# A two-block network on one core: low parts of a projection moved to VectorE, the experts' sums started from the residual, a semaphore for the number of rounds

## The reference

```python
# block 1, behind its first feed-forward (D_FF 2816)
h = rms_norm(x, norm_mix)
p = h @ w_in                       # 1024 x 3328; the last 1792 columns are u
# RWKV-7 mix of those columns
u = u + (token_shift(u) - u) * mu  # token_shift: the row of the token before, zeros ahead
...
# block 2, behind its attention: x is the residual, t its norm
y = sum over 16 experts: gate_e * ((silu(t @ w1e) * (t @ w3e)) @ w2e)   # 2 of 16 per token
x = x + g * y                      # g: a row of 1024 gates from the modulation
out = x * rsqrt(mean(x * x) + 1e-6) * final_g
```

## Time and profile before

| | |
|---|---|
| Median of 3 runs | 1210.21 us (1205.83 to 1211.66) |
| Profiled execution | 1211.14 us, its span 1209.3 us |
| Mean granted TensorE clock | 0.982 of full |
| TensorE busy | 1146.7 us (95%) |
| VectorE busy | 604.2 us (50%) |
| ScalarE busy | 446.9 us (37%) |
| GpSimd busy | 51.6 us (4%) |
| HBM read | 252.25 MB |

### The profile page before, as it was taken

The page is one execution under the profiler, slowest core; times in us unless marked ns, Lnnn a source line. Parts: engine busy times, 40 slices in busy tenths (PEclk is TensorE's granted clock), DMA queues, the critical chain, the costliest instruction groups (busy, mean ns, idle before and its releaser), DMA issues.

```text
span 1209.3 us, 20587 instructions
## 1 busy us (share of the span) xinstructions
PE 1146.7 (95%) x8864; PEld 922.0 (76%) x8864; DVE 604.2 (50%) x767; ACT 446.9 (37%) x532; POOL 51.6 (4%) x37
## 2 busy tenths in 40 slices
PE   6999998998989998999999999999979799999996
PEld 6999997997768747999999999888878544444443
DVE  5544546798534275654456481477486511111114
ACT  6333345752441125434335242466553411111112
POOL 0000000340032000000000000000000000000000
PEclk9999999998999999999999999999999899999998
DMA  9655556452664743655654352433225799999991
GB/s 342 213 175 188 194 177 190 140 166 82 231 255 142 272 166 121 196 187 177 200 179 139 105 175 71 140 105 105 73 97 183 278 364 423 421 421 421 421 422 56
DMA packets 119845, 254.32 MB, mean 210 GB/s; under 512 B 6097, under 2 KB 91361, under 8 KB 107234
## 3 DMA queue, kind: packets, MB, share of 16 engines
q1 hardware_dynamic: 118578, 248.61, 57.6%
q10 hardware_dynamic: 1200, 4.71, 1.1%
HBM read 252.25 MB, written 1.06 MB: 209 GB/s over the span
## 4 chain that ended last, share of the span: by engine, by line
PE 87%; DVE 7%; ACT 3%; issue 1%; DMA 1%; SPq 0%; DVEq 0%; ACTq 0%
PE ps L652 52%; PE ps L633 33%; ACT arena L1309 2%; DMA ring<-in_ffn_gate 1%; DVE ring_r L1804 1%; PE ps L1101 1%; ACT arena_r L1309 1%; DVE arena L2074 1%; DVE arena L1950 1%; ACT L1309 1%; DVE arena L1946 1%; DVE arena L1951 0%; DVE arena L1956 0%; DVE arena L1962 0%; PE ps L640 0%
## 5 line engine op out<-in xcount | busy, mean ns | idle before, releaser
L652 PE MATMUL ps<-hall_r,arena_r 128*128 128x256 f32 x1664 | 301.3, 283 | 2.9 <-DVE hall_r L1810 2.9
L1804 DVE TENSOR_TENSOR ring_r<-ring,arena_r 128x2048 fp32r<-128x2048 f32 x90 | 205.9, 2291 | 194.0 <-ACT arena_r L1309 191.9
L652 PE MATMUL ps<-arena_r 128*128 128x256 f32 (+1 forms) x1280 | 290.1, 322 | 7.4 <-DVE ring_r L1804 4.2
L652 PEld LDWEIGHTS ps<-hall_r,arena_r 128*128 128x128 f32 x1664 | 257.7, 189 | 5.1 <-issue 2.1
L1309 ACT ACTIVATE arena_r<-ring 128x2048 fp32r<-128x2048 f32 x100 | 190.6, 1914 | 159.8 <-PE ps L652 153.7
L652 PE MATMUL ps<-hall_r,ring_r 128*128 128x256 f32 x880 | 247.5, 281 | 0.0
L1309 ACT ACTIVATE arena<-ps 128x512 f32<-128x512 f32 (+4 forms) x147 | 86.1, 597 | 409.5 <-PE ps L652 211.0
L652 PEld LDWEIGHTS ps<-arena_r 128*128 128x128 f32 x1280 | 211.3, 189 | 26.2 <-DVE ring_r L1804 4.4
L633 PE MATMUL ps<-arena 64*64 64x32 f32 (+7 forms) x2360 | 204.7, 301 | 3.7 <-issue 1.5
L633 PEld LDWEIGHTS ps<-arena 128*64 128x64 f32 (+3 forms) x2360 | 135.7, 146 | 72.8 <-issue 62.8
L652 PEld LDWEIGHTS ps<-hall_r,ring_r 128*128 128x128 f32 x880 | 169.0, 192 | 0.9
(11 more groups left out here) (228 smaller groups left out, 922.5 us busy)
## 6 DMA issues: line engine op xcount, KB each, us to landing
ring<-in_w_in SPq DMA_DIRECT2D x35, 1024.0 KB, 5.2
ring<-in_w_exp_gate SPq DMA_DIRECT2D x32, 1024.0 KB, 11.6
arena<-in_w_exp_down SPq DMA_DIRECT2D x32, 1024.0 KB, 11.2
ring<-in_w_mod SPq DMA_DIRECT2D x24, 1024.0 KB, 5.6
ring<-in_ffn_gate SPq DMA_DIRECT2D x22, 1024.0 KB, 5.4
ring<-in_ffn_up SPq DMA_DIRECT2D x22, 1024.0 KB, 5.3
ring<-in_ffn_down SPq DMA_DIRECT2D x22, 1024.0 KB, 5.0
ring<-in_w_exp_up SPq DMA_DIRECT2D x16, 1024.0 KB, 14.1
```

Source lines behind the costliest of these rows:

```text
L652: m = pe.matmul(out_, w[i], h[j], start=start and i + j == 0, stop=stop and j == 1, skip_group_check=group)
L1804: tt(lo(n), slot(n), hi(n), ALU.subtract).then_inc(S("w_lo"), 1)
```

## The change

Three things, and what they bring with them.

- **Projection.** All thirteen low parts are VectorE's. `copy_out(j)` for j < 7 now writes (1 - mu) times the bank into the target tile, in two operations of 256 columns, with `mu_rest` = 1 - mu made once at the start; `shift(j)` adds mu times the bank's columns, one to the left, straight from PSUM. `ubuf` and `ushift` go. TensorE therefore also waits for `shift(j - 4)` before it writes a bank again. Two high parts have other places, and high parts 8 and 9 another order on ScalarE.
- **Residual.** The four clearing matmuls become four with the identity and x, so the banks start from x. `y_e` is multiplied by g as it is copied, in two operations on VectorE; ScalarE's copy goes. The scatter goes half by half of the columns and signals each of its four banks. ScalarE squares each bank as it is ready, VectorE's final product reads the banks, and the final gain comes by a broadcast DMA into `gb[:, 0]`, issued on SP behind the first pair's loads. Each half of the output is stored when it is ready.
- **Rounds.** "rounds" leaves the group `dve_tail` and has a semaphore of its own.

```diff
--- before.py
+++ after.py
@@ -169,15 +169,15 @@
             "pe_rms": [("sbo_ms", 2), ("y_mean", 2), ("y_var", 2)],
-            "pe_tail": [("dft_1", 4), ("heads_ss", 4), ("dft_2", 2), ("route_bias", 1), ("logits_t", 2), ("logits", 1), ("places", 2), ("moe_sum", 2),
-                        ("final_gain", 1)],
+            "pe_tail": [("dft_1", 4), ("heads_ss", 4), ("dft_2", 2), ("route_bias", 1), ("logits_t", 2), ("logits", 1), ("places", 2), ("moe_sum", 4),
+                        ],
...
                          ("route_w", 1), ("route_shift", 1), ("n5_inv", 2),
-                         ("route_max", 1), ("chosen", 1), ("route_diff", 1), ("tables", 10), ("rounds", 1)],
+                         ("route_max", 1), ("chosen", 1), ("route_diff", 1), ("tables", 10)],
@@ -297,7 +297,7 @@
-            block = (23, 21, 17, 25, None, 23, 25, None, 25, None, 7, 25, 5)[j]
+            block = (23, 21, 17, 25, None, 23, 25, None, 4, 25, 7, None, 5)[j]
@@ -372,8 +372,13 @@
         x_wa, x_g, t_w, s_g = (A(3, 256, 256 * j) for j in range(4))
-        ubuf = A(4, 1028).rearrange("p (b f n) -> p b f n", b=2, f=2)
-        ushift = A(4, 512, 1028).rearrange("p (f n) -> p f n", f=2)
+        mu_rest = small[:, 56:70]
...
+        def mixed(j, f):
...
+            tile = 2 * RW_ORDER[j] + f
+            return {12: x_wa, 13: x_g}.get(tile, rw_x[tile // 4 * 4][:, tile % 4, :] if tile < 12 else None)
@@ -402,6 +407,7 @@
         w_end = small[:, 0:16].rearrange("p (k c) -> p k c", k=4)
+        halves_ss, half_mean = small[:, 0:4], small[:, 4:6]
@@ -552,14 +558,16 @@
             expert_pair(0, 0, True)
+            sp.wait_ge(*W("x4_done", 4))
+            sp.dma_start(gb[:, 0, :], a["rows"][:, 0:D].broadcast_to([P, D])).then_inc(S("final_gain"), 16)
...
                 expert_pair((i % (E // 2)) * 2, i)
-            sp.wait_ge(*W("final", 2))
             for t in range(TT):
+                sp.wait_ge(*W("final", t + 1))
@@ -579,12 +587,6 @@
             pool.memset(r_scan.rearrange("p (c n) -> p c n", n=CH)[:, :, 0:1], 0.0).then_inc(S("reset_mask"), 1)
...
-            pool.memset(ubuf[:, :, :, 0:1], 0.0).then_inc(S("ubuf_zero"), 1)
-            for j in range(5, 10):
-                pool.wait_ge(*W("win_hi", j + 1))
-                pool.tensor_tensor(lo_cols(N_WIN + j), cols(N_WIN + j), win_hi(j), ALU.subtract).then_inc(
-                    S("win_lo_p"), 1)
@@ -614,9 +616,8 @@
             pool.wait_ge(*W("w_used", N_AO + 2))
-            pool.memset(y_e, 0.0).then_inc(S("y_kept_v"), 1)
+            pool.memset(y_e, 0.0).then_inc(S("y_kept_v"), 2)
             pool.memset(pick_t, 0.0).then_inc(S("pick_t"), 1)
-            pool.memset(zero_blk, 0.0).then_inc(S("zeros"), 1)
@@ -759,12 +760,11 @@
                 n = N_WIN + j
-                if 5 <= j < 10:
-                    pe.wait_ge(*W("win_lo_p", j - 4))
-                else:
-                    pe.wait_ge(*W("win_lo_v", j + 1 if j < 5 else j - 4))
+                pe.wait_ge(*W("win_lo_v", j + 1))
...
                     pe.wait_ge(*W("win_copied", j - 3))
+                if 4 <= j < 11:
+                    pe.wait_ge(*W("shifted", j - 3))
@@ -1206,9 +1206,10 @@
-            pe.wait_ge(*W("zeros", 1))
-            for b in range(4):
-                m = mm(ps[:, 4 + b, :], zero_blk, cst[:, 0:512], stop=False, group=True)
+            pe.wait_ge(*W("x4_done", 4))
+            for t in range(TT):
+                for h in range(2):
+                    m = mm(ps[:, 4 + 2 * t + h, :], ident, x[:, t, h * 512:(h + 1) * 512], stop=False, group=True)
@@ -1222,15 +1223,14 @@
-                pe.wait_ge(*W("y_kept_v", i + 1))
-                pe.wait_ge(*W("y_kept_a", i + 1))
                 pe.wait_ge(*W("pick_t", i + 1))
-                for t in range(TT):
-                    for h in range(2):
+                for h in range(2):
+                    pe.wait_ge(*W("y_kept_v", i * 2 + (h + 1)))
+                    for t in range(TT):
...
                                stop=False, group=True)
-                    if sem:
-                        m.then_inc(S(sem), 1)
+                        if sem:
+                            m.then_inc(S(sem), 1)
@@ -1267,8 +1267,7 @@
                 pe.wait_ge(*W("picked", i + 2))
-                pe.wait_ge(*W("y_kept_v", i + 1))
-                pe.wait_ge(*W("y_kept_a", i + 1))
+                pe.wait_ge(*W("y_kept_v", i * 2 + 2))
@@ -1298,10 +1297,6 @@
-            for h in range(2):
-                m = mm(ps[:, h, :], ones[0:1, :], row_f[:, h * 512:(h + 1) * 512])
-            m.then_inc(S("final_gain"), 1)
@@ -1410,12 +1405,14 @@
                 if j < 7:
-                    if j >= 2:
-                        act.wait_ge(*W("shifted", j - 1))
-                    elif j == 0:
-                        act.wait_ge(*W("ubuf_zero", 1))
-                    o = ubuf[:, j % 2, :, 1:T + 1]
-                elif j < 11:
+                    if j == 0:
+                        act.wait_ge(*W("mu_rest", 1))
+                    for g in range(2):
+                        tile = 2 * RW_ORDER[j] + g
+                        m = f(mixed(j, g), bank[:, g, :], ACT.Copy, scale=mu_rest[:, tile:tile + 1])
+                    m.then_inc(S("win_copied"), 1)
+                    return
+                if j < 11:
@@ -1455,13 +1452,13 @@
             high_in(7)
+            high_in(8)
...
             copy_out(6)
-            high_in(8)
+            high_in(9)
             copy_out(7)
-            high_in(9)
@@ -1743,8 +1740,6 @@
-            act.wait_ge(*W("y_kept_v", 1))
-            act.sem_inc(S("y_kept_a"), 1)
@@ -1763,17 +1758,22 @@
                 f(hs_t, ps[:, 0, :].rearrange("p (k n) -> p k n", k=4), ACT.Copy).then_inc(S("hs_t"), 1)
-                act.wait_ge(*W("w_used", i * 12 + (N_EXP + 12)))
-                f(y_e[:, 0:512], ps[:, 2, :], ACT.Copy).then_inc(S("y_kept_a"), 1)
...
             fetch(ACT.Sqrt)
-            for t in range(TT):
-                act.wait_ge(*W("x5_done", 2 * (t + 1)))
-                f(gated[:, t, :], x[:, t, :], ACT.Square, accum_out=ssum[:, t:t + 1]).then_inc(S("n6_ss"), 1)
-                act.wait_ge(*W("n6_ss", t + 1))
-                f(rstd[:, t:t + 1], ssum[:, t:t + 1], ACT.Sqrt, scale=1.0 / D, bias=EPS_COL).then_inc(
-                    S("n6_root"), 1)
...
+            for h in range(2):
+                for t in range(TT):
+                    n = 2 * h + t + 1
+                    act.wait_ge(*W("moe_sum", n))
+                    f(gated[:, t, h * 512:(h + 1) * 512], ps[:, 4 + 2 * t + h, :], ACT.Square,
+                      accum_out=halves_ss[:, 2 * h + t:2 * h + t + 1]).then_inc(S("n6_ss"), 1)
+                    act.wait_ge(*W("n6_ss", n))
+                    if h == 0:
+                        f(half_mean[:, t:t + 1], halves_ss[:, t:t + 1], ACT.Identity, scale=1.0 / D,
+                          bias=EPS_COL).then_inc(S("n6_mean"), 1)
+                    else:
+                        act.wait_ge(*W("n6_mean", t + 1))
+                        f(rstd[:, t:t + 1], halves_ss[:, 2 + t:3 + t], ACT.Sqrt, scale=1.0 / D,
+                          bias=half_mean[:, t:t + 1]).then_inc(S("n6_root"), 1)
@@ -1863,6 +1863,9 @@
             split(N_FFN1)
+            v.wait_ge(*W("vec_in", 16))
+            ts(mu_rest, vec[:, VEC_AT["rw_mu"][0]:VEC_AT["rw_mu"][0] + 14], -1.0, 1.0, ALU.mult, ALU.add).then_inc(
+                S("mu_rest"), 1)
@@ -1909,16 +1912,10 @@
                 v.wait_ge(*W("win_copied", j + 1))
-                if j:
-                    v.wait_ge(*W("shifted", j))
-                u = ubuf[:, j % 2, :, 1:T + 1]
-                link(tt(ushift, ubuf[:, j % 2, :, 0:T], u, ALU.subtract))
-                for f in range(2):
-                    tile = 2 * RW_ORDER[j] + f
-                    o = {12: x_wa, 13: x_g}.get(tile)
-                    if o is None:
-                        o = rw_x[tile // 4 * 4][:, tile % 4, :]
-                    m = stt(o, ushift[:, f, :], V("rw_mu", tile), u[:, f, :], ALU.mult, ALU.add)
+                for g in range(2):
+                    tile = 2 * RW_ORDER[j] + g
+                    o = mixed(j, g)[:, 1:T]
+                    m = stt(o, ps[:, j % 4, g * T:g * T + T - 1], V("rw_mu", tile), o, ALU.mult, ALU.add)
@@ -1931,6 +1928,7 @@
             shift(2)
+            low_in(5)
@@ -1940,7 +1938,9 @@
             shift(3)
+            low_in(6)
             shift(4)
+            low_in(7)
@@ -1954,6 +1954,8 @@
             tt(k_bar, kf, w_inv, ALU.mult).then_inc(S("k_bar"), 1)
+            low_in(8)
+            low_in(9)
@@ -2231,17 +2233,12 @@
-            def add_gated(tag, gate, b0, used=None):
...
-                for t in range(TT):
-                    v.wait_ge(*(W("moe_sum", t + 1) if used is None else W("w_used", used) if t else
-                                W("tile_0", 4)))
-                    for h in range(2):
-                        s = slice(h * 512, (h + 1) * 512)
```

(20 more changed lines are left out.)

## The result

The changed kernel takes 1193.84 us (median of 4 runs, 1192.80 to 1195.26) against 1210.93 for the kernel before (4 runs on the same chip, 1205.83 to 1212.35): a ratio of 0.9867, 95% interval 0.9835 to 0.9899, so 17.1 us less where 17.0 were forecast. Its profiled execution took 1192.80 us with a span of 1191.0, 18.3 less than the 1209.3 of before.

The account below looks back on a forecast made before the run. The prediction took TensorE to bound the kernel. Gains of 7.3 (projection), 6.4 (rounds) and 3.5 (tail), less 0.15, made 17.0 us; 1211.14 less that and less 0.9 gave 1193.2 us, range 1188 to 1200.

Parts of the forecast that it names:

- Projection: Projection: low parts on VectorE and PSUM reads shorten TensorE's waits, gain 7.3 us, bounds 4 and 9.
- The 62 more cycles: Projection: a skill table's extra fixed cost for PSUM sources, 0.9 us over 14 reads; the forecast followed the rows instead.
- rival B: Projection: project(9) waits longer and the clock drops, gain 2 to 4 us in place of 7.3; chance 0.15.
- The wait for shift(5): Projection: new TensorE wait of 2.1 us before project(9), because VectorE now reads the PSUM bank it writes.
- Rounds: Experts' start: own semaphore gains 6.4 us, 3.6 from an earlier start and 2.85 from the clock.
- The open question: Experts' start: matmuls begin at 957.6 if reading the number overlaps the gather, 958.9 if not; 958.2 taken.
- The 2.85: Experts' start: us saved because TensorE's clock stays up once its idle time shrinks, bounds 0 and 2.85.
- C: Experts' start: it does not move, or the clock falls anyway after thin routing; gain there 0 to 3 us; chance 0.08.
- Tail: After the last scatter: shorter chain gains 3.0 us and the earlier first store 0.5, together 3.5, bounds 2.5 and 4.5.
- Hidden edits: Residual and gate: identity matmuls and the loop's second VectorE product cost 0, hidden behind other work.
- D: Expert loads: slower broadcast and late loads take back the experts' gain, time up to 1199.6 us; chance 0.06.
- The estimate of 3.6: Final gain's 512 KB broadcast DMA: 3.6 us, half its nearest row's 7.2; 1.2 by its bytes.

Follow-up runs that it names:

- e5: The changed kernel with low parts 5 to 9 back on GpSimd, the PSUM reads kept: 1194.10 us, 0.9851 of the kernel before.
- e2: The kernel before with only the projection's part changed: 1205.01 us, 0.9951 of the kernel before.
- e10: The changed kernel run again, unaltered, beside others on the same chip: 1194.28 us, 0.9865 of the kernel before.
- e8: The changed kernel with both output stores issued only behind the second final product: 1195.33 us, 0.9860 of the kernel before.
- e1: The kernel before with only the semaphore of the number of rounds changed: 1204.38 us against 1210.54, 0.9944.
- e3: The kernel before with only the residual's part changed: 1205.48 us, 0.9951 of the kernel before.
- e4: The kernel before with four unread matmuls of 448 columns behind the first gather, the wait for rounds kept: 1207.95 us against 1210.54, 0.9976.
- e6: The kernel before with all low parts on VectorE, shift and ubuf as they were: 1205.68 us, 0.9947 of the kernel before.
- e9: The changed kernel with two unread matmuls of 512 columns ahead of project(9)'s wait for shift(5): 1194.74 us, 0.9860 of the kernel before.
- e11: The changed kernel with VectorE's list in the order TensorE asks for things, run a second time: 1186.54 us, 0.9808 of the kernel before.

## Why the prediction was right, and where its terms were off

**Projection: right, 7.5 for 7.3.** The dates worked out from VectorE's list held to 0.3 us: low 7 done at 247.2, maximum begun at 249.06, low 8 done at 263.4, shift(5) at 271.3, bonus_v at 275.35. So did the reading of the long operations as contention. (The forecast's text counts "four products and k_bar" behind the reciprocal; the list has three and k_bar, and its sum, 261.2, used those four.) In e5 the contention came back when GpSimd's subtractions did, and e5 adds a finding: the RECIPROCAL was not held up by the next subtraction, the TENSOR_SCALAR was. The Trainium skill, "GPSIMD Engine Reference", section 1 (the table of interfaces), names besides two SBUF inputs the VectorE instructions in a 2-port mode; the Trainium skill, "VectorE: DVE Perf Modes", section "Mode 2×_2P", counts a float32 `tensor_scalar` from SBUF among these. The TENSOR_SCALAR's rows, 5.12 against 0.69, agree with that; for a RECIPROCAL the section gives no mode, and its 6.55 both times stands as measured. A PSUM read cost nothing extra: 0.44 for each of two at 243.12. The 62 more cycles that the forecast took from the Trainium skill, "VectorE: DVE Perf Modes", did not show.

**Half of rival B happens, at times.** The wait for shift(5) was forecast at 2.1 and is 1.9. Of four profiles that hold it, two show the clock drop behind it (e2 and e10) and two do not (the change, and e8, whose projection's length is 92.8 as well). Nothing in the lists differs between e10 and the first profile. But the two with the drop are also the two with the low start, so that the wait falls about 1.3 us later in them; what the clock did in the first 15 us of the projection thus seems to decide it, which no run was made to show. The forecast gave the drop 0.15, with a gain of only 2 to 4 us; it came in two of four profiles, its price was 1.5 us (it had put the losses at 5.2 with a drop and 3.5 without), and the length fell by 4.8 and 4.6 us even so. The medians presumably hold some of both.

**A give-back that was not foreseen.** Of the 7.5 won by 301, 6.8 are left at the second feed-forward and 6.5 at the gather. One place is seen: the stretch from 330 to 340 ran at 0.66. The length from gram to the second feed-forward was 161.2 to 162.3 in the five profiles with the old `shift` (before, e1, e3, e4, e6) and 162.9 to 163.3 in the five with the changed projection (the change, e2, e8, e9, e10), whose stretch from 330 to 340 ran at 0.66 to 0.77. So the loss of 0.8 comes with the change and not with one execution; how it comes about is open.

**Rounds: right, 7.0 in the profile and 6.2 alone for 6.4.** The open question, whether reading the number into a register overlaps the gather, was put at 0.6 us of gap and is answered by none. From the gather's start to the first expert matmul it was 8.10 and is 3.77, so the wait's term is 4.3, a hair past its upper bound of 4.2, and the rest of the 7.0, 2.6, is the clock's. The 2.85 was too high because the low clock was read as lasting until 967.6; views of 0.2 us show it full again from 967.2. C falls: e1 and e4 show that the idle time makes the clock fall and that the thin stretch ahead of it does not.

**Tail: the term for the store was too small.** The shorter chain was forecast at 3.0 and measured at 3.5, since ScalarE takes 0.9 a half (1182.10, 1183.02, 1183.92) where 1.1 was put together from other rows. The store was given 0.5; the span fell by 18.3, the end of the final product by 17.0, so it brought 1.35, and e8's trace gives the same 1.3. The first store's issue and the start of its transfer now lie beside the second final product.

**Hidden edits stayed hidden.** The loop's period is 28.61 us before and after, so the second product on `y_e` costs nothing, and TensorE waits for no load in the last pairs. D had its condition without its effect: the broadcast took 18.8 us to land, behind pair 0's loads, and the last pair's up tiles 20.2, where they took 20.0.

```profile
gb<-in_rows SPq DMA_DIRECT2D x1, 512.0 KB, 18.8
```
```profile
arena<-in_w_exp_up SPq DMA_DIRECT2D x2, 1024.0 KB, 20.2
```

The estimate of 3.6 for that broadcast did not hold in a full queue, and no run shows it alone; the first final product needs it only at 1185.22, 227 us after it landed. `mu_rest`'s 0.15 was not to be seen. The sum of the profile, 18.3, is thus 7.5 - 1.05 + 7.0 + 3.5 + 1.35: the terms of rounds and tail came out larger, by 0.6 and 1.35, and the give-back took 1.05 away. The agreement of the medians (17.1 for 17.0) is thus in part luck: the profiled execution of the change was 1.0 us faster than the median of its runs, errors of about a microsecond cancelled, and the runs of one kernel lie several microseconds apart.

## What to carry to other kernels

Where events share a semaphore, a wait on the last of them waits for all: take out of the group any event on which another engine's loop begins. Before giving work to GpSimd, look at the rows of VectorE that run beside it, and price them by their own rows elsewhere. An edit that reads PSUM in place of a copy ties the bank to the reader, so the reader's list has to be put in the order in which TensorE asks for banks: the reordered list was 8 us faster here, half as much as the whole change, though only 4.2 to 5.7 of that lie in the projection itself.

## What the runs showed of the hardware

A register read of TensorE's that waits on a semaphore costs no gap while matmuls are queued ahead of it, and 1.2 to 1.3 us when none are left (1.3 in the earlier trace rows, 1.24 in e4). A VectorE operation with one input in SBUF can be held up by GpSimd sevenfold (0.69 to 5.12 us), another with one input not at all (RECIPROCAL, 6.55 both times). The same idle time of 1.9 us brought TensorE's clock from 2.4 to 1.2 GHz in two executions and left it in two others, at a price of 1.5 us. Executions of the same kernel on the same chip lie up to 10 us apart (1183.09 to 1193.31 in e11, 1190.87 to 1198.88 in e10).
